# The start of a hybrid attention, convolution and expert block: small loads between tiles of x, first transposes over six banks

## The chip, the cores and the metric

The kernel runs on one core of one Trainium2 chip. The metric is the device time of one execution in microseconds (us). Three executions of the kernel before took 1255.04, 1256.41 and 1256.52 us; the median is 1256.41.

## What is computed

The input x has 512 rows of 1024 float32. With random weights, one layer computes:

```python
h = rmsnorm(x, g_mix)
proj = h @ w_in                      # 1024 x 4608: q | k | v | GLU input | branch gates
o = diff_attention(q, k, v, lam, rel_bias)      # 4 heads, two softmax maps each, chunk-causal
u = glu_a * sigmoid(glu_b); u = silu(layernorm(depthwise_conv31(u)))
merged = gate_A * (rmsnorm(o) @ w_attn_up) + gate_B * (u @ w_conv_pw2 + b_conv_pw2)
x = x + merged @ w_out
x = x + hier_moe(rmsnorm(x, g_ffn))  # 64 experts: top group of 8, top 2 of 8 in it, SwiGLU
out = rmsnorm(x, g_final)
```

## The kernel before

The five engines and their queues have programs of their own, each in a fixed order written by hand, and they meet by semaphores. x lies in four tiles of 128 rows by 1024. A dense part (projection, attention, convolution, merge, output projection) comes first, then the expert part, which streams the weights of the experts (2 MB for each of gate, up and down) through three places in SBUF. These places overlap memory that the dense part uses, so the first loads of expert weights wait for tiles of the dense part; `load_first(0, 0)` waits for the last tile of the output projection.

The change is in the first 30 us. What happens there, engine by engine:

- SP (L565 on) issues the loads: four tiles of x (L568), then six small vectors (`VEC_ROWS`: g_mix, b_conv_pw2, b_dw, g_conv_ln, b_conv_ln, g_subln) into `rows29` (L573), the convolution taps `w_dw` (L575) and `rel_bias` (L576). Then the first chunk of w_in, `glu_b` (2 MB, L587), the rest of `consts` (L589), four lambda vectors (L591) and the second chunk, `glu_a`. All of it is one queue. ACT issues the identity, `consts[:, 0:P]`, itself (L751).
- VectorE and ScalarE compute the mean square of two tiles of x each (L1026, L759), ScalarE the roots (L764), VectorE the scaled rows `xn` (L1032, `xn_ready`).
- TensorE (L1497 on) waits for the identity and for all eight small loads, transposes the small vectors and taps (tile `vec`, L1500 and L1502), which VectorE copies to `vec` and `taps` (L1041 to L1045). Then it transposes `xn` into hT: eight columns of 128 features, each four transposes of 128 by 128, one PSUM bank for a column (tile `xT`, c). Columns 0 and 1 are done tile by tile as `xn` comes (L1518), columns 2 to 7 one after the other (L1524). The banks rotate over three (`NBANK`, `open_tile`): tile n of the plan `PLAN` takes bank n % 3 and waits until tile n - 3 has been copied out. After column 5 stand the two bias rows (`bias_rows`, L1508 to L1512), which need `consts` and `rel_bias` and write into the two banks of `ps_s`.
- ScalarE copies each column, times g_mix and rounded, to `hT` (L783, `hT_high`); after column 2 stands `high_part(0)`, which rounds the first piece of `glu_b` (L777) and waits for its load. `high_part(1)` and the copy of the bias rows follow after column 7.
- VectorE computes the remainder `hT_low` of each column (L1049), which frees the bank.
- GpSimd subtracts the rounded piece of weights from the raw one (L693, `w_split`).
- TensorE then runs the projection tiles (`split_columns`, matmuls at L1492): for each 24 matmuls of 128 x 128 by 128 x 512, in three passes (high times high, low times high, high times low), eight columns in each. The first tile (n == 0) waits column by column.

After the eight GLU tiles come the strips of the bias, q, k, v, then the gates between the steps of the attention.

Of the kernel before, what the change touches and what calls it, by code (L numbers as in the profile page):

```python
# [30 lines left out]
ALU = mybir.AluOpType  # L31
# [3 lines left out]
P = 128  # L35
# [121 lines left out]
def plan():  # L157

    tiles = [("vec", 0)]
    tiles += [("xT", c) for c in range(KD)]  # L160
    tiles += GLU + [("strip", h) for h in range(HEADS)]
    tiles += [("q", m) for m in range(HEADS)] + [("k", m) for m in range(HEADS)]
    tiles += [("v", t) for t in range(T)]
    for m in range(2 * KD):
        tiles.append(("gate", m))
        if m == 5:
            tiles.append(("mean", 0))
        if m == 8:
            tiles.append(("var", 0))
    tiles += [("yc", 0), ("yc", 1)] + [("oT", h) for h in range(HEADS)]  # L170
    for m in range(KD):
        tiles += [("yc", m + 2)] * (m < KD - 2) + [("ya", m)]
    for t in range(T):
        tiles += [("out", 2 * t), ("out", 2 * t + 1)]
        if t:
            tiles += [("hT", 2 * t - 2), ("hT", 2 * t - 1)]
    tiles += [("hT", 2 * T - 2), ("hT", 2 * T - 1)]
    return tiles
# [52 lines left out]
def block_kernel(nc, a, out):  # L231
# [5 lines left out]
    with ExitStack() as ctx:  # L237
# [174 lines left out]

        def xT_bank(n):
            return (pair_a, pair_b)[n // 2 % 2][:, n % 2, :]
# [7 lines left out]
        in_const, in_const2, in_small, in_bcast = sem("in_const"), sem("in_const2"), sem("in_small"), sem("in_bcast")  # L422
        in_x = [sem(f"in_x{t}") for t in range(T)]
# [142 lines left out]
        def _(sp):  # L566
            for t in range(T):
                sp.dma_start(x[:, t, :], ap("x")[0, t * P:(t + 1) * P, :]).then_inc(in_x[t], 16)  # L568
# [7 lines left out]
            sp.dma_start(rb_sb[:, :], ap("rel_bias")).then_inc(in_small, 16)  # L576
# [166 lines left out]
        def _(act_e):  # L743
# [37 lines left out]
            for c in range(KD):  # L781
                tile_ready(act_e, "xT", c)
                act_e.activation(hT[:, c, :], bank_of("xT", c)[:, :], ACT.Copy,  # L783
                                 scale=vec[:, VEC["g_mix"] + c:VEC["g_mix"] + c + 1]).then_inc(hT_high, 1)
                if c == 2:
                    high_part(0)
# [225 lines left out]
        def _(dve):  # L1012
# [24 lines left out]
            for t in range(1, T):  # L1037
                scale_x(t)
# [8 lines left out]
            for c in range(KD):  # L1047
                dve.wait_ge(hT_high, c + 1)
                dve.scalar_tensor_tensor(out=hT_low[:, c, :], in0=bank_of("xT", c)[:, :],  # L1049
                                         scalar=vec[:, VEC["g_mix"] + c:VEC["g_mix"] + c + 1], in1=hT[:, c, :].bitcast(F32),  # L1050
                                         op0=ALU.mult, op1=ALU.subtract).then_inc(copied("xT", c), 1)
# [412 lines left out]
        def _(pe):  # L1464
# [9 lines left out]
            def split_columns(kind, m, n):  # L1474

                dst = open_tile(kind, m)
                name, j = PIECES[n]
# [6 lines left out]
                for i, (w, rows) in enumerate(passes):  # L1484
                    if n == 0 and i == 1:
                        pe.wait_ge(w_split, 1)
                    for c in range(KD):
                        if n == 0 and i == 0:
                            pe.wait_ge(hT_high, c + 1)
                        if n == 0 and i == 2:  # L1490
                            tile_out(pe, "xT", c)
# [6 lines left out]
            pe.wait_ge(in_small, 16 * (len(VEC_ROWS) + 2))  # L1498
# [7 lines left out]
            def bias_rows():  # L1506

                pe.wait_ge(in_const2, 16)  # L1508
                at, w = CONST["bucket"]
# [4 lines left out]
            first = [open_tile("xT", c) for c in range(2)]  # L1514
            for t in range(T):
                pe.wait_ge(xn_ready, t + 1)
                for c in range(2):
                    last = pe.transpose(first[c][:, t * P:(t + 1) * P], xn[:, t, c * P:(c + 1) * P], ident)  # L1518
                    if t == T - 1:
                        last.then_inc(tile_done, 1)  # L1520
            for c in range(2, KD):
                dst = open_tile("xT", c)
                for t in range(T):
                    last = pe.transpose(dst[:, t * P:(t + 1) * P], xn[:, t, c * P:(c + 1) * P], ident)  # L1524
                last.then_inc(tile_done, 1)
                if c == 5:
                    bias_rows()
# [395 lines left out]
```

## Time and profile before

| | |
|---|---|
| median of three executions | 1256.41 us (1255.04 to 1256.52) |
| the profiled execution | 1256.11 us, span 1254.3 us |
| PE (matmul) busy | 1116.5 us, 89% of the span |
| DVE busy | 562.6 us, 45% |
| ACT busy | 271.4 us, 22% |
| POOL busy | 143.0 us, 11% |
| DMA | 408.83 MB, mean 326 GB/s |

The span runs from the first to the last instruction of the profiled execution. PE is TensorE's matmul, PEld its weight load, DVE VectorE, ACT ScalarE, POOL GpSimd, SPq the issue of DMAs by SyncE. Busy shares are means over a program whose parts have different limits: in the first slice PE waits for its inputs, then it is busy almost without a break, and in the later two thirds of the span DMA moves around 425 GB/s.

### The profile page before, as it was taken

How to read it: one execution, taken by the hardware profiler on the slowest of the kernel's cores; microseconds unless marked ns; L12 is line 12 of the kernel's file. 1: busy time of each engine (PE TensorE's matmuls, PEld its weight loads, DVE VectorE, ACT ScalarE, POOL GpSimd, SP SyncE). 2: the span in 40 equal slices, each digit the busy share in tenths (PEclk: the TensorE clock that was granted, in tenths of full speed). 3: DMA queues.
4: the chain of work that ended last, by engine and by line, in shares of the span. 5: the costliest groups of instructions: out<-in, count | busy, mean ns of one | idle time of the engine just before them, and what ended most of it. 6: DMA issues, size and time to landing. Idle time of an engine off the chain costs nothing.

```text
span 1254.3 us, 29895 instructions
## 1 busy us (share of the span) xinstructions
PE 1116.5 (89%) x12369; PEld 684.0 (55%) x12370; DVE 562.6 (45%) x1176; ACT 271.4 (22%) x683; POOL 143.0 (11%) x84
## 2 busy tenths in 40 slices
PE   5999999999999987689997999997998877796886
PEld 4878777768885544345553555544554433353444
DVE  3799433545245542334443444443443433242342
ACT  4133234385132110111111111111111111011112
POOL 2454543246100000000000000000000000000000
PEclk9999999999999998889998999998999989898899
DMA  6333111153159999999999999999999999999995
GB/s 238 118 99 114 68 67 68 68 201 125 78 206 370 425 422 424 426 427 381 393 426 425 426 425 425 424 425 425 427 425 426 426 425 425 423 426 427 425 423 239
DMA packets 51309, 408.83 MB, mean 326 GB/s; under 512 B 6410, under 2 KB 6567, under 8 KB 21066
## 3 DMA queue, kind: packets, MB, share of 16 engines
q1 hardware_dynamic: 50778, 407.22, 78.4%
q0 software_dynamic: 352, 1.06, 0.3%
q8 instruction: 25, 0.41, 0.1%
q10 hardware_dynamic: 144, 0.07, 0.0%
q14 instruction: 10, 0.08, 0.0%
HBM read 406.22 MB, written 2.11 MB: 326 GB/s over the span
## 4 chain that ended last, share of the span: by engine, by line
DMA 64%; PE 29%; ACT 2%; DVE 2%; issue 1%; SPq 1%; DVEq 0%; ACTq 0%
DMA sb_weights<-in_w_exp_up 60%; PE ps_all L1492 13%; DMA sb_weights<-in_w_exp_gate 3%; PE ps_all L1736 2%; PE ps_all L1543 2%; PE ps_all L1670 1%; PE ps_all L1674 1%; PE ps_all L1667 1%; DMA sb_consts<-in_consts 1%; PE ps_all L1622 1%; PE ps_all L1795 1%; PE ps_all L1628 1%; PE ps_all L1625 1%; PE ps_all L1557 1%; PE ps_all L1863 1%
## 5 line engine op out<-in xcount | busy, mean ns | idle before, releaser
L1736 PE MATMUL ps_all<-sb_weights,sb_late 128*32 128x256 f32 x4608 | 306.4, 421 | 89.2 <-DMA sb_weights<-in_w_exp_up 87.8
L1736 PEld LDWEIGHTS ps_all<-sb_weights,sb_late 128*32 128x32 f32 x4608 | 168.2, 117 | 218.9 <-issue 133.7
L1397 DVE TENSOR_TENSOR sb_late<-sb_late,ps_all 128x128 f32<-128x128 f32 x72 | 20.7, 288 | 392.9 <-ACT sb_late L970 392.9
L1392 DVE TENSOR_TENSOR sb_x<-sb_x,ps_all 128x512 f32<-128x512 f32 x184 | 114.1, 682 | 105.1 <-PE ps_all L1795 105.1
L1749 PE MATMUL ps_all<-sb_weights,sb_late 128*32 128x256 f32 x2304 | 139.2, 382 | 0.4 <-ACT sb_late L974 0.4
L1717 PE MATMUL ps_all<-sb_hT,sb_late 128*32 128x256 f32 x2304 | 138.5, 380 | 0.6 <-DVE sb_late L1266 0.6
L1492 PE MATMUL ps_all<-sb_hT_r,sb_ring_r 128*128 128x512 f32 x512 | 124.0, 394 | 0.0
L1492 PEld LDWEIGHTS ps_all<-sb_hT_r,sb_ring_r 128*128 128x128 f32 x512 | 94.8, 188 | 26.8 <-issue 6.5
L1717 PEld LDWEIGHTS ps_all<-sb_hT,sb_late 128*32 128x32 f32 x2304 | 75.7, 109 | 61.0 <-issue 17.4
L1749 PEld LDWEIGHTS ps_all<-sb_weights,sb_late 128*32 128x32 f32 x2304 | 67.5, 109 | 63.3 <-issue 25.6
L970 ACT ACTIVATE sb_late<-ps_all 128x128 f32<-128x128 f32 x72 | 20.0, 278 | 366.7 <-PE ps_all L1736 366.7
L1795 PE MATMUL ps_all<-sb_g_ffn,sb_late 32*128 32x512 f32 x736 | 87.2, 587 | 0.0
L693 POOL TENSOR_TENSOR sb_ring_r<-sb_ring,sb_ring_r 128x1024 fp32r<-128x1024 f32 x32 | 76.3, 2394 | 66.5 <-ACT sb_ring_r L777 65.5
L1064 DVE SCALAR_TENSOR_TENSOR ps_all<-sb_work,sb_taps,ps_all 128x512 f32<-128x512 f32 x116 | 79.7, 749 | 1.2
L962 ACT ACTIVATE sb_late<-ps_all 128x256 f32<-128x256 f32 x72 | 27.7, 384 | 176.9 <-PE ps_all L1717 176.9
L980 ACT ACTIVATE sb_late<-ps_all 128x256 f32<-128x256 f32 x72 | 27.7, 385 | 173.6 <-PE ps_all L1749 173.6
L1492 PE MATMUL ps_all<-sb_x_r,sb_ring_r 128*128 128x512 f32 x256 | 63.2, 389 | 0.0
L1795 PEld LDWEIGHTS ps_all<-sb_g_ffn,sb_late 32*128 32x128 f32 x736 | 37.7, 185 | 41.3 <-issue 41.3
L1381 DVE SCALAR_TENSOR_TENSOR ps_all<-sb_late,sb_consts 128x512 f32<-128x512 f32 x72 | 54.2, 753 | 0.0
L1492 PEld LDWEIGHTS ps_all<-sb_x_r,sb_ring_r 128*128 128x128 f32 x256 | 48.1, 188 | 10.0
L1795 PE MATMUL ps_all<-sb_router_w,sb_late 32*128 32x512 f32 x368 | 52.5, 640 | 0.0
L1724 PE MATMUL ps_all<-sb_consts,sb_late 128*128 128x128 f32 x144 | 31.4, 300 | 17.0 <-ACT sb_late L962 16.8
(307 smaller groups left out, 1058.7 us busy)
## 6 DMA issues: line engine op xcount, KB each, us to landing
sb_weights<-in_w_exp_up SPq DMA_DIRECT2D x59, 2048.0 KB, 14.6
sb_weights<-in_w_exp_down SPq DMA_DIRECT2D x59, 2048.0 KB, 14.5
sb_weights<-in_w_exp_gate SPq DMA_DIRECT2D x59, 2048.0 KB, 14.5
sb_ring<-in_w_in SPq DMA_DIRECT2D x9, 2048.0 KB, 9.0
sb_x<-in_x SPq DMA_DIRECT2D x8, 512.0 KB, 5.1
sb_ring<-in_w_conv_pw SPq DMA_DIRECT2D x1, 2048.0 KB, 9.1
sb_ring<-in_w_attn_up SPq DMA_DIRECT2D x1, 2048.0 KB, 7.8
sb_ring<-in_w_out SPq DMA_DIRECT2D x1, 2048.0 KB, 12.8
```

Source lines behind the costliest of these rows:

```text
L693: pool.tensor_tensor(w_low[name][:, :, j * P:(j + 1) * P], raw, high.bitcast(F32), ALU.subtract).then_inc(w_split, 1)
L962: act_e.activation(rows_sb, ps_rows[:, 0:QCOLS], ACT.Copy).then_inc(rows_ready, 1)
L980: act_e.activation(y_sb[c], ps_y[:, 0:QCOLS], ACT.Copy).then_inc(y_ready, 1)
L1064: dve.scalar_tensor_tensor(out=dst, in0=pad[:, c, k:k + SEQ], scalar=taps[:, c, k:k + 1], in1=conv_sum[c], op0=ALU.mult, op1=ALU.add).then ...
L1381: dve.scalar_tensor_tensor(out=ps_second, in0=d_list[:, 1, :], scalar=slot_at, in1=w_list[:, 1, :], op0=ALU.is_equal, op1=ALU.mult).then_i ...
L1392: ins = dve.tensor_tensor(rows, rows, banks[g].rearrange("p (t s) -> p t s", t=T), ALU.add)
L1492: last = mm(dst[:, :], w[:, c, :], rows[:, c, :], start=i + c == 0, stop=i == 2 and c == KD - 1)
L1717: last = mm(ps_rows[g * BLK:(g + 1) * BLK, 0:QCOLS], onehots[c][:, t, :], h2[:, t, g * QCOLS:(g + 1) * QCOLS], start=t == 0, stop=t == T - 1)
L1724: last = pe.transpose(ps_hTb[:, c * P:(c + 1) * P], rows_sb[:, c * P:(c + 1) * P], ident)
L1736: last = mm(ps_gu[g * BLK:(g + 1) * BLK, 0:2 * P].rearrange("p (a n) -> p a n", a=2), rows, weights[:, at:at + 3:2, r % 4, cols], start=r ...
L1749: last = mm(ps_y[g * BLK:(g + 1) * BLK, 0:QCOLS], actT[:, k * BLK:(k + 1) * BLK], weights[:, 6 * c + 4 + k // 2, k % 2 * 2 + g // 2, g % 2 ...
L1795: last = mm(banks[g], y_sb[j][rows, half * P:(half + 1) * P], w_rows[j][rows, :], start=j == 0, stop=j == NBUF - 1)
```

## The change

Three things are moved. SP issues x0 and x1, then the six vectors and the taps, then x2, x3 and rel_bias, which gets a semaphore of its own (`in_rb`). The transposes of x no longer belong to the plan of rotating tiles: six columns have a bank each (`hx_bank`), and the transposes of columns 0 to 5 run tile by tile as `xn` comes; columns 6 and 7 follow in the banks of columns 0 and 1 once these are lowered (`hT_lowered`). Semaphores `hx_done` and `hT_lowered` take the place of the tile counters. `bias_rows` stands after all the transposes and waits for `in_rb` and for `hT_lowered` 5, since columns 3 and 4 lie in the banks that it writes. The second projection tile waits for `hT_lowered` 8. All later tiles of the plan have numbers lower by eight, so their banks are others.

```diff
--- before.py
+++ after.py
@@ -157,7 +157,6 @@
 def plan():
 
     tiles = [("vec", 0)]
-    tiles += [("xT", c) for c in range(KD)]
     tiles += GLU + [("strip", h) for h in range(HEADS)]
     tiles += [("q", m) for m in range(HEADS)] + [("k", m) for m in range(HEADS)]
     tiles += [("v", t) for t in range(T)]
@@ -410,6 +409,8 @@
             return pairs[t].rearrange("p a n -> p (a n)")
 
 
+        hx_bank = [ps_t, ps_o, ps_oT, ps_s[:, 0, :], ps_s[:, 1, :], bank[2], ps_t, ps_o]
+
         def xT_bank(n):
             return (pair_a, pair_b)[n // 2 % 2][:, n % 2, :]
 
@@ -420,6 +421,7 @@
 
 
         in_const, in_const2, in_small, in_bcast = sem("in_const"), sem("in_const2"), sem("in_small"), sem("in_bcast")
+        in_rb, hx_done, hT_lowered = sem("in_rb"), sem("hx_done"), sem("hT_lowered")
         in_x = [sem(f"in_x{t}") for t in range(T)]
         in_ring = [sem(f"in_ring{i}") for i in range(NRING)]
         in_router = sem("in_router")
@@ -564,7 +566,7 @@
 
         @block.sync
         def _(sp):
-            for t in range(T):
+            for t in range(2):
                 sp.dma_start(x[:, t, :], ap("x")[0, t * P:(t + 1) * P, :]).then_inc(in_x[t], 16)
             at = 0
             for name, rows in VEC_ROWS:
@@ -573,7 +575,9 @@
                 sp.dma_start(rows29[at:at + rows, :], ap(src)[0].rearrange("(r p) -> r p", p=P)).then_inc(in_small, 16)
                 at += rows
             sp.dma_start(taps_row, ap("w_dw")[0]).then_inc(in_small, 16)
-            sp.dma_start(rb_sb[:, :], ap("rel_bias")).then_inc(in_small, 16)
+            for t in range(2, T):
+                sp.dma_start(x[:, t, :], ap("x")[0, t * P:(t + 1) * P, :]).then_inc(in_x[t], 16)
+            sp.dma_start(rb_sb[:, :], ap("rel_bias")).then_inc(in_rb, 16)
             for n, name in enumerate(CHUNKS):
                 before = [c for c in CHUNKS[:n] if PLACE[c] == PLACE[name]]
                 if name == "up":
@@ -779,8 +783,8 @@
 
             act_e.wait_ge(vec_ready, 1)
             for c in range(KD):
-                tile_ready(act_e, "xT", c)
-                act_e.activation(hT[:, c, :], bank_of("xT", c)[:, :], ACT.Copy,
+                act_e.wait_ge(hx_done, c + 1)
+                act_e.activation(hT[:, c, :], hx_bank[c], ACT.Copy,
                                  scale=vec[:, VEC["g_mix"] + c:VEC["g_mix"] + c + 1]).then_inc(hT_high, 1)
                 if c == 2:
                     high_part(0)
@@ -1034,7 +1038,8 @@
             square_x(0)
             scale_x(0)
             square_x(2)
-            for t in range(1, T):
+            scale_x(1)
+            for t in range(2, T):
                 scale_x(t)
 
             tile_ready(dve, "vec", 0)
@@ -1046,9 +1051,9 @@
 
             for c in range(KD):
                 dve.wait_ge(hT_high, c + 1)
-                dve.scalar_tensor_tensor(out=hT_low[:, c, :], in0=bank_of("xT", c)[:, :],
+                dve.scalar_tensor_tensor(out=hT_low[:, c, :], in0=hx_bank[c],
                                          scalar=vec[:, VEC["g_mix"] + c:VEC["g_mix"] + c + 1], in1=hT[:, c, :].bitcast(F32),
-                                         op0=ALU.mult, op1=ALU.subtract).then_inc(copied("xT", c), 1)
+                                         op0=ALU.mult, op1=ALU.subtract).then_inc(hT_lowered, 1)
 
             dve.wait_ge(in_bcast, 64)
             for j in range(2):
@@ -1474,6 +1479,8 @@
             def split_columns(kind, m, n):
 
                 dst = open_tile(kind, m)
+                if n == 1:
+                    pe.wait_ge(hT_lowered, KD)
                 name, j = PIECES[n]
                 low, high = w_low[name][:, :, j * P:(j + 1) * P], high_of(n)
                 passes = [(high, hT), (low, hT), (high, hT_low)]
@@ -1488,14 +1495,14 @@
                         if n == 0 and i == 0:
                             pe.wait_ge(hT_high, c + 1)
                         if n == 0 and i == 2:
-                            tile_out(pe, "xT", c)
+                            pe.wait_ge(hT_lowered, c + 1)
                         last = mm(dst[:, :], w[:, c, :], rows[:, c, :],
                                   start=i + c == 0, stop=i == 2 and c == KD - 1)
                 last.then_inc(tile_done, 1)
 
 
             pe.wait_ge(in_const, 16)
-            pe.wait_ge(in_small, 16 * (len(VEC_ROWS) + 2))
+            pe.wait_ge(in_small, 16 * (len(VEC_ROWS) + 1))
             dst = open_tile("vec", 0)
             pe.transpose(dst[:, 0:NVEC], rows29, ident[0:NVEC, 0:NVEC])
             for c in range(KC):
@@ -1506,25 +1513,25 @@
             def bias_rows():
 
                 pe.wait_ge(in_const2, 16)
+                pe.wait_ge(in_rb, 16)
+                pe.wait_ge(hT_lowered, 5)
                 at, w = CONST["bucket"]
                 mm(ps_s[0:HEADS, 0, :], rb_sb[:, :], consts[0:BUCKETS, at:at + SEQ], start=True, stop=True)
                 mm(ps_s[0:HEADS, 1, 0:P], rb_sb[:, :], consts[0:BUCKETS, at + SEQ:at + w], start=True, stop=True)\
                     .then_inc(rb_done, 1)
 
-            first = [open_tile("xT", c) for c in range(2)]
             for t in range(T):
                 pe.wait_ge(xn_ready, t + 1)
-                for c in range(2):
-                    last = pe.transpose(first[c][:, t * P:(t + 1) * P], xn[:, t, c * P:(c + 1) * P], ident)
+                for c in range(6):
+                    last = pe.transpose(hx_bank[c][:, t * P:(t + 1) * P], xn[:, t, c * P:(c + 1) * P], ident)
                     if t == T - 1:
-                        last.then_inc(tile_done, 1)
-            for c in range(2, KD):
-                dst = open_tile("xT", c)
+                        last.then_inc(hx_done, 1)
+            for c in range(6, KD):
+                pe.wait_ge(hT_lowered, c - 5)
                 for t in range(T):
-                    last = pe.transpose(dst[:, t * P:(t + 1) * P], xn[:, t, c * P:(c + 1) * P], ident)
-                last.then_inc(tile_done, 1)
-                if c == 5:
-                    bias_rows()
+                    last = pe.transpose(hx_bank[c][:, t * P:(t + 1) * P], xn[:, t, c * P:(c + 1) * P], ident)
+                last.then_inc(hx_done, 1)
+            bias_rows()
 
             for n, (name, m) in enumerate(GLU):
                 split_columns(name, m, n)
```

## Rows read from the trace of the kernel before

**Rows 1.** The page, part 4: shares of the chain that ended last.

```profile
DMA 64%; PE 29%; ACT 2%; DVE 2%; issue 1%; SPq 1%; DVEq 0%; ACTq 0%
```

**Rows 2.** The chain in time (start us, us, what), 0 to 70, then 345 to 420.

```profile
6.33 12.82 DMA sb_consts<-in_consts
...
21.46 43.56 PE ps_all L1492 x192
...
359.52 7.68 DMA sb_weights<-in_w_exp_gate
```

**Rows 3.** Timeline (start us, us, engine, line, ...), SP's DMA issues.

```profile
0.72 1.82 SPq L568 DMA_DIRECT2D sb_x<-in_x  x4
...
2.58 0.40 SPq L573 DMA_DIRECT2D sb_late<-in_g_mix  x1
...
5.21 0.25 SPq L575 DMA_DIRECT2D sb_late<-in_w_dw  x1
...
5.87 0.42 SPq L587 DMA_DIRECT2D sb_ring<-in_w_in  x1
```

**Rows 4.** The same timeline, ScalarE.

```profile
6.16 1.06 ACT L759 ACTIVATE sb_dense<-sb_x 128x1024 f32<-128x1024 f32 x1 [3.40 <-DMA sb_x<-in_x]
...
9.17 1.06 ACT L759 ACTIVATE sb_dense<-sb_x 128x1024 f32<-128x1024 f32 x1 [1.49 <-DMA sb_x<-in_x]
...
14.73 1.84 ACT L783 ACTIVATE sb_hT_r<-ps_all,sb_vec 128x512 fp32r<-128x512 f32 x3 [4.04 <-PE ps_all L1518]
...
17.13 1.06 ACT L777 ACTIVATE sb_ring_r<-sb_ring 128x1024 fp32r<-128x1024 f32 x1 [0.56 <-DMA sb_ring<-in_w_in]
18.10 1.83 ACT L783 ACTIVATE sb_hT_r<-ps_all,sb_vec 128x512 fp32r<-128x512 f32 x3
...
21.06 1.27 ACT L783 ACTIVATE sb_hT_r<-ps_all,sb_vec 128x512 fp32r<-128x512 f32 x2 [1.13 <-PE ps_all L1524]
```

**Rows 5.** The same timeline, VectorE and TensorE.

```profile
11.60 0.75 DVE L1032 TENSOR_SCALAR sb_dense<-sb_x,sb_small 128x1024 f32<-128x1024 f32 x1
...
12.24 0.28 PE L1500 MATMUL ps_all<-sb_consts,sb_late 29*128 29x29 f32 x1 [12.24 <-DMA sb_rb_sb<-in_rel_bias]
...
12.88 1.97 PE L1518 MATMUL ps_all<-sb_consts,sb_dense 128*128 128x128 f32 x8
12.98 0.19 DVE L1041 COPY sb_vec<-ps_all 128x29 f32<-128x29 f32 x1 [0.63 <-PE ps_all L1502]
...
18.80 2.07 DVE L1049 SCALAR_TENSOR_TENSOR sb_x_r<-ps_all,sb_vec,sb_hT_r 128x512 fp32r<-128x512 f32 x3 [1.28 <-ACT sb_hT_r L783]
...
19.20 1.02 PE L1510 MATMUL ps_all<-sb_consts,sb_rb_sb 32*4 32x512 f32 x2 [0.69 <-DMA sb_consts<-in_consts]
...
20.36 1.09 PE L1524 MATMUL ps_all<-sb_consts,sb_dense 128*128 128x128 f32 x8
...
21.21 3.92 PE L1492 MATMUL ps_all<-sb_hT_r,sb_ring_r 128*128 128x512 f32 x16
...
26.78 3.79 PE L1492 MATMUL ps_all<-sb_hT_r,sb_ring_r 128*128 128x512 f32 x16
...
32.22 3.79 PE L1492 MATMUL ps_all<-sb_hT_r,sb_ring_r 128*128 128x512 f32 x16
```

**Rows 6.** Timeline of TensorE alone, batches of 64 in the expert loop.

```profile
471.46 5.45 PE L1736 MATMUL ps_all<-sb_weights,sb_late 128*32 128x256 f32 x64 [4.96 <-DMA sb_weights<-in_w_exp_up]
...
486.25 6.60 PE L1736 MATMUL ps_all<-sb_weights,sb_late 128*32 128x256 f32 x64 [4.81 <-DMA sb_weights<-in_w_exp_up]
...
950.23 5.11 PE L1736 MATMUL ps_all<-sb_weights,sb_late 128*32 128x256 f32 x64 [4.41 <-DMA sb_weights<-in_w_exp_up]
...
1201.65 5.46 PE L1736 MATMUL ps_all<-sb_weights,sb_late 128*32 128x256 f32 x64 [4.05 <-DMA sb_weights<-in_w_exp_up]
```

**Rows 7.** Windows: us, busy us of each engine, granted clock, DMA share, GB/s.

```profile
471.46:476.90 5.44, 5.44 (x68) 3.27 (x72) 0.00 (x0) 0.00 (x0) 0.00 (x0) 0.69 1.02 429
...
570.21:574.06 3.85, 3.85 (x68) 2.37 (x68) 0.00 (x0) 0.39 (x1) 0.00 (x0) 1.00 0.97 409
```

## The prediction

> **What bounds the kernel now.** I read the shares of the chain of waits first, then the chain in order of time, then the timeline of the first 50 us. By shares the chain is 64% DMA and 29% PE [rows 1]: the experts' weights stream at the DMA limit, the dense part before them is TensorE. In order of time [rows 2] the chain has the load of consts until 19.15, and then PE without a break: 43.56 us of projection matmuls from 21.46 on. Where the output matmuls end, at 359.52, the chain passes to the first load of expert weights, and from there it is nearly all transfers. So what the change does to the moment at which PE gets through the first projection tile is passed on in full: PE has no idle time that could absorb it, and the stream of weights starts when PE's dense work ends. The routing is by data, so the number of loads stays.
>
> In the first 27 us, four engines work side by side [rows 3 to 5]. SP issues four tiles of x, seven small loads and rel_bias, then glu_b at 5.87. PE stands until 12.24 for the last small load, then transposes. ACT starts copying hT at 14.73, does three columns, waits for glu_b until 17.13, splits its first piece (1.06), and goes on. PE meets consts at 19.20 (two bias rows), transposes the last two columns at 20.36, starts the first projection tile at 21.21 and the second at 26.78, where an undisturbed tile takes 32.22 - 26.78 = 5.44.
>
> **The change part by part.**
>
> *Small loads between x1 and x2.* Two x issues take 0.91 of the 1.82; the small ones run from 2.58 to 5.46 (2.88 us). So x2 is issued at about 4.5 instead of 1.6 and x3 at 5.0 instead of 2.1; rel_bias and glu_b keep their place, as do consts, the lambdas and the next chunk behind them. Do x2 and x3 land later? x1 landed at 6.16 and x3 at 9.17 [rows 4], 1.5 us a tile, so the queue was still at x1 when x2 will be issued. Nothing is later at the lower end; at the upper end the full 2.88 us. I take 0 (the row of x1 is near, and the bytes ahead of glu_b are the same), 0.5 being possible. The small loads are then in at about 7.5 and the vec transposes leave the path; before, they stood at 12.24 with 0.64 us to the first transpose.
>
> *Six banks, tile by tile.* VectorE gives the last tile of x at 11.60 + 0.75 = 12.35 [rows 5], and the vec copies queued behind it, 0.38 us from 12.98 on, end at about 12.75. With eight transposes in 1.76 us (12.88 to 14.64), 0.22 each, six cost 1.3 a tile; the first three tiles lie beside VectorE's work, the last ends at 13.2 to 14.4, and column 0 is ready at 12.9 to 13.5 instead of 14.73. So ACT starts 1.2 to 1.8 us earlier. That gain is worth nothing: after three columns (until 14.7 to 15.3) ACT's next instruction in order is the split of glu_b, whose transfer still lands at 17.1, and columns 3 to 7 are queued behind it. What is gained there is one later stall: ACT no longer waits 1.13 us for columns 6 and 7 (21.06), so columns 3 to 7 run 18.10 to 21.1 at 0.60 each instead of ending at 22.33.
>
> *bias_rows behind all transposes, with a new wait for hT_lowered 5.* Columns 3 and 4 are in banks of ps_s. VectorE lowers column 3 from 18.80 and column 4 by 18.80 + 2 x 0.69 = 20.18. So the bias rows, now the last thing ahead of the first projection, start at 20.2 instead of 19.20. Queued behind the wait are the whole projection stream and everything that depends on it. They take 1.16 us (19.20 to 20.36), and the first projection starts at 21.36, not 21.21: +0.15. The two columns of transposes (0.85) that stood between now lie beside ACT. The first tile took 5.57 before, with small stalls for columns 6 and 7; these columns are now ready, and it takes 5.44: -0.13. Sum so far 0.0. The added wait of the second projection tile for hT_lowered 8 (about 21.9) is long met at 26.8; renumbering the tiles moves their banks by one and keeps the distance of three.
>
> *PE idles before the bias rows.* Its last transposes (column 7, after VectorE lowered column 1) end at 15.6 to 16.6, the next work is at 20.2: 3.6 to 4.6 us of idle time where the kernel before waited 0.69. What such a gap does is shown in the expert loop [rows 6, 7]: a batch of 64 matmuls takes 3.85 at a granted clock of 1.00 (570.21), but 5.45 after 4.96 us of idle (471.46), with a mean clock of 0.69, so part of it runs at 1.2 instead of 2.4 GHz. There are 17 such batches, the first at 471.46 and the last at 1201.65, each after 4.05 us of idle or more; the shortest is 5.11, the longest 6.60, their mean 5.62. No gap of 4.05 us or more was free of it. The bias rows and the first projection tile are such dense work, so the loss is 1.3 to 2.8 us, by the mean 1.8. This is the only term of size. Lower end: nothing, if the gap is too short.
>
> The transposes before were at full speed by 20.36: eight in 1.09 there against 1.97 at 12.88, though they had nothing but transposes ahead [rows 5]. The Trainium skill (TensorE: Matmul & The Clock Gate, Part 4: PE-mode transpose) says that transposes do not count as activity for the full clock. By that rule the first projection tile of the kernel before would have started at 1.2 GHz as well, the change would lose nothing new, and the sum would be 0.0. The trace does not agree: 16 projection matmuls from 21.21 on took 3.92 us, about the 3.8 of the later tiles.
>
> Sum: 0.0 + 1.8 on the profiled execution's 1256.11 (span 1254.3 and 1.8 around it) is 1257.9; that execution is 0.3 under the median shown, 1256.41, so 1258.2.
>
> **The rivals.**
>
> A, the forecast: all gains hidden behind glu_b, +1.8 from the clock. 1258.2, own range 1257.5 to 1259.5.
>
> B, the clock stays up. The gap can be 3.6 us, shorter than any that the trace shows to cost. Then nothing changes in sum: 1256.4. For it: the length. Against: every gap only half a microsecond longer had it fall [rows 6], and the transposes ahead of this one leave PE idle between tiles as well. This is also what the skill's rule on transposes would give.
>
> C, slower: the late x2 and x3 are the bound. If the queue runs dry between x1 and x2, x3 slips by up to 2.88 us. From 1.8 us of slip on (17.13 less the 15.3 at which ACT ends three columns) this decides also without the loads behind it; what glu_b and consts slip counts in full from the first tenth. With all of it 1256.4 + 2.9 + 1.8 = 1261.1, with a slip of 1 us 1259.2. Against: DMA was still delivering x1 at 6.16.
>
> D, faster: glu_b or consts land earlier because fewer small packets stand in their way at that time. ACT then starts its split at 15.3 instead of 17.13, columns 3 to 7 end at 19.3, bias rows start at 18.4, 1.8 us earlier, after an idle time too short for the clock: 1254.6. For it: ACT and PE really are ready earlier, so this is the one thing that would cash the 1.2 to 1.8 us. Against: the same bytes stand ahead of glu_b in the same queue.
>
> **How the numbers follow.** About 0.2%, 2.5 us, is what a measurement of this kernel can tell from no change. A 0.55, B 0.2, C 0.13, D 0.12. The likeliest gives 1258.2. The range 1255.0 to 1260.5 leaves out the ends of C and D. Slower by over 0.2% (above 1258.9): a quarter of A, the long cold stretches, and nearly all of C, 0.25. Faster (below 1253.9): half of D and some chance on top for a mechanism that I do not see, 0.08. Same: 0.67. The expert loop adds its own scatter of a microsecond or so: the batch at 1201.65, near the end, is one of those that took from 5.11 to 6.60.
>
> **What would show it.** The vec transposes before 9 us; the first hT activation at 13 to 13.5, three of them, then the wait for glu_b to about 17.1; columns 3 to 7 in one run to 21.1; bias rows at about 20.2 after 3.6 us or more of idle PE; the first 16 projection matmuls in 5 us or more, not 3.92; the second projection tile at 28.5, not 26.78; the first load of expert weights at 361.3, not 359.52. Full clock in these 16 matmuls means B. x3 landing after 9.7 or glu_b after 17.6 means C, glu_b before 16.5 means D. The forecast is wrong if the second tile starts before 27 or after 30, or if the load of expert weights does not move with it.

## The result, and the profile after

The changed kernel takes 1260.48 us (median of 8 executions, 1258.77 to 1261.06), the kernel before 1256.21 (8 executions, 1254.53 to 1256.93). The ratio is 1.0029 with a 95% interval of 1.0020 to 1.0038: slower by 4.3 us by the medians, clear of noise. The profiled execution has a span of 1257.5 us, 3.2 more than before.

The chain in order of time (start us, us, what), from the start and around 360 us. Where [rows 2] had the load of consts, there is now the load of x2; from it the chain goes on over VectorE, the transposes and ScalarE to column 4 on VectorE (ready at 20.56) and the bias rows. The projection block that took 43.56 takes 46.32; the first load of expert weights stands at 362.88 instead of 359.52.

```profile
3.97 6.21 DMA sb_x<-in_x
...
22.55 46.32 PE ps_all L1499 x192
...
362.88 7.74 DMA sb_weights<-in_w_exp_gate
```

SP's issues, which answer to [rows 3]. The seven small loads now stand between 1.64 and 3.97; x2 and x3 follow. The seven issues take 2.29 us here and took 2.88 before, where one of them alone had 0.73, so x2 goes out 0.5 us earlier than counted.

```profile
0.72 0.87 SPq L570 DMA_DIRECT2D sb_x<-in_x  x2
...
1.64 0.37 SPq L575 DMA_DIRECT2D sb_late<-in_g_mix  x1
...
3.97 0.83 SPq L579 DMA_DIRECT2D sb_x<-in_x  x2
```

ScalarE, answering to [rows 4]. The second tile that ACT squares is in hand at 11.51 instead of 9.17, the first three columns of hT start at 15.74 instead of 14.73, the split of glu_b follows them without a wait at 17.46 (17.13 before), and the five other columns run in one piece.

```profile
11.51 1.06 ACT L763 ACTIVATE sb_dense<-sb_x 128x1024 f32<-128x1024 f32 x1 [4.29 <-DMA sb_x<-in_x]
...
15.74 1.85 ACT L787 ACTIVATE sb_hT_r<-ps_all,sb_vec 128x512 fp32r<-128x512 f32 x3 [2.71 <-PE ps_all L1526]
...
17.46 1.06 ACT L781 ACTIVATE sb_ring_r<-sb_ring 128x1024 fp32r<-128x1024 f32 x1
18.41 3.01 ACT L787 ACTIVATE sb_hT_r<-ps_all,sb_vec 128x512 fp32r<-128x512 f32 x5
```

VectorE and TensorE, answering to [rows 5]. The vec transposes come 3 us earlier (9.25), but the last tile of xn only at 13.94 + 0.75 = 14.69 (12.35 before). After column 7 (its last transpose ends at 18.57) PE is idle for 2.12 us until VectorE has lowered column 4. Then the bias rows take 1.42 instead of 1.02, and 16 projection matmuls take 6.49 instead of 3.92. The second tile starts at 30.63 instead of 26.78, the third 5.44 later, as before.

```profile
9.25 0.28 PE L1507 MATMUL ps_all<-sb_consts,sb_late 29*128 29x29 f32 x1 [9.25 <-DMA sb_late<-in_w_dw]
...
13.94 0.75 DVE L1036 TENSOR_SCALAR sb_dense<-sb_x,sb_small 128x1024 f32<-128x1024 f32 x1
...
17.26 1.31 PE L1532 MATMUL ps_all<-sb_consts,sb_dense 128*128 128x128 f32 x8 [0.56 <-DVE sb_x_r L1054]
...
19.14 3.38 DVE L1054 SCALAR_TENSOR_TENSOR sb_x_r<-ps_all,sb_vec,sb_hT_r 128x512 fp32r<-128x512 f32 x5 [0.61 <-ACT sb_hT_r L787]
...
20.70 1.42 PE L1519 MATMUL ps_all<-sb_consts,sb_rb_sb 32*4 32x512 f32 x2 [2.12 <-DVE sb_x_r L1054]
...
22.48 6.49 PE L1499 MATMUL ps_all<-sb_hT_r,sb_ring_r 128*128 128x512 f32 x16
...
30.63 3.79 PE L1499 MATMUL ps_all<-sb_hT_r,sb_ring_r 128*128 128x512 f32 x16
...
36.07 3.79 PE L1499 MATMUL ps_all<-sb_hT_r,sb_ring_r 128*128 128x512 f32 x16
```

Windows of the same execution (busy us of PE, PEld, DVE, ACT, POOL, then granted clock, DMA share, GB/s). Before the bias rows PE is busy for 0.58 of 2.70 us. In the first projection tile the granted clock is 0.50, that is 1.2 GHz, and in the third window it comes back. Narrower windows put the fall at about 21.2, inside the bias rows, and the return at 28.0.

```profile
18.00:20.70 2.70, 0.58 (x7) 0.37 (x6) 2.09 (x4) 2.70 (x6) 2.09 (x1) 1.00 0.93 351
22.48:26.00 3.52, 3.52 (x9) 2.81 (x9) 2.50 (x5) 0.74 (x2) 2.40 (x1) 0.50 0.39 146
26.00:29.00 3.00, 3.00 (x10) 2.38 (x9) 0.00 (x0) 2.00 (x2) 1.08 (x1) 0.67 0.01 2
```

### The profile page after: what moved, and what is told of

The parts are those of the page before. It is cut to its first block, busy times and chain, and to the rows that moved or that the text cites. A ratio compares the mean times of both kernels' runs of the same rounds, so it can differ in the third digit from the quotient of the medians.

```text
span 1257.5 us, 29896 instructions
## 1 busy us (share of the span) xinstructions
PE 1119.4 (89%) x12369; PEld 685.5 (55%) x12370; DVE 564.5 (45%) x1176; ACT 271.3 (22%) x683; POOL 143.0 (11%) x84
## 3 DMA queue, kind: packets, MB, share of 16 engines
HBM read 406.22 MB, written 2.11 MB: 325 GB/s over the span
## 4 chain that ended last, share of the span: by engine, by line
DMA 64%; PE 29%; DVE 2%; ACT 2%; issue 1%; SPq 1%; POOL 0%; DVEq 0%; ACTq 0%
DMA sb_weights<-in_w_exp_up 60%; PE ps_all L1499 13%; DMA sb_weights<-in_w_exp_gate 3%; PE ps_all L1743 2%; PE ps_all L1550 2%; PE ps_all L1677 1%; PE ps_all L1681 1%; PE ps_all L1674 1%; PE ps_all L1632 1%; PE ps_all L1802 1%; PE ps_all L1635 1%; PE ps_all L1629 1%; PE ps_all L1564 1%; PE ps_all L1870 1%; PE ps_all L1756 1%
## 5 line engine op out<-in xcount | busy, mean ns | idle before, releaser
L1499 PE MATMUL ps_all<-sb_hT_r,sb_ring_r 128*128 128x512 f32 x512 | 126.6, 400 | 0.0
```

The lines of the kernel that those rows point to most:

```text
L1499: last = mm(dst[:, :], w[:, c, :], rows[:, c, :], start=i + c == 0, stop=i == 2 and c == KD - 1)
```

## The experiments

Each was timed beside the kernel before. A useful mark is the start of the second projection tile: from there to the first load of expert weights the twelve profiles have 332.2 to 333.6 us, whatever was changed ahead of it, and from that load to the end 893.8 to 895.7.

```
kernel                    median   ratio to before (95%)     2nd tile  expert load
before                    1256.2                             26.78     359.52
changed                   1260.5   1.0029 (1.0020-1.0038)    30.63     362.88
e1 loads only             1258.3   1.0014 (1.0005-1.0023)    27.54     361.10
e2 banks only             1260.6   1.0034 (1.0022-1.0047)    31.59     363.93
e3 gap filled             1257.0   1.0003 (0.9994-1.0012)    27.57     360.91
e4 small loads on ACT     1264.6   1.0061 (1.0047-1.0075)    33.48     367.00
e5 bias rows later        1256.6   0.9999 (0.9990-1.0008)    26.87     359.42
e6 before, bias later     1257.2   1.0006 (0.9997-1.0014)    27.50     360.04
e7 x first, vec later     1256.8   0.9999 (0.9990-1.0008)    26.93     360.19
e8 e7, reordered, filled  1258.0   1.0009 (1.0000-1.0018)    27.16     360.40
e9 gaps filled in place   1254.3   0.9982 (0.9973-0.9991)    25.44     357.85
e10 e9 without filling    1257.9   1.0009 (1.0000-1.0018)    26.86     359.91
```

The medians are of several sessions; the kernel before had medians of 1256.2 to 1257.0 in them, so the ratios are what to compare. The two marks are of one profiled execution each, and that need not be a typical one: between the changed kernel and e3 the second tile moves by 3.06 us, the load of expert weights by 1.97 and the ratio by 0.0026, which is 3.3 us.

**e1: only the order of the loads**, in the kernel before.

```diff
-            for t in range(T):
+            for t in range(2):
                 sp.dma_start(x[:, t, :], ...)
...
+            for t in range(2, T):
+                sp.dma_start(x[:, t, :], ...)
+            sp.dma_start(rb_sb[:, :], ap("rel_bias")).then_inc(in_rb, 16)
```

> The kernel before with only the order of the loads changed (x0, x1, small, x2, x3, rel_bias); banks, transposes and bias rows as before. Theory (late x and a half-rate clock together make the loss, the clock the larger part): the last tile of xn comes at about 14.7 instead of 12.35, column 0 of hT at 15.7 or so, bias rows at 19.2 to 20, PE has no gap of 2 us ahead of them, the clock stays up; the second projection tile starts at 27.0 to 27.8, and the time is 0.3 to 1.2 us above the kernel before. Rival (the order of the loads is the whole loss): 3 to 4 us above it. Second rival (the clock falls in any case): the first 16 projection matmuls take 5 us or more.

Measured: 1.0014, second tile at 27.54, 0.76 later than before. Its timeline:

```profile
15.29 1.84 ACT L786 ACTIVATE sb_hT_r<-ps_all,sb_vec 128x512 fp32r<-128x512 f32 x3 [2.29 <-PE ps_all L1522]
...
16.82 2.82 PE L1528 MATMUL ps_all<-sb_consts,sb_dense 128*128 128x128 f32 x12 [0.50 <-DVE sb_x_r L1052]
...
19.57 1.40 PE L1514 MATMUL ps_all<-sb_consts,sb_rb_sb 32*4 32x512 f32 x2
...
21.97 3.92 PE L1495 MATMUL ps_all<-sb_hT_r,sb_ring_r 128*128 128x512 f32 x16
...
27.54 3.79 PE L1495 MATMUL ps_all<-sb_hT_r,sb_ring_r 128*128 128x512 f32 x16
```

Column 0 starts at 15.29 and not at 14.73, because x2 and x3 are late here too. PE has almost no gap, and the 16 projection matmuls take 3.92. But twelve transposes from 16.82 on take 2.82, and the bias rows at 19.57 still 1.40, where they took 1.02 at 19.20 before: with the early work spread thin the clock also came up later. The bias rows start 0.37 later and their first product takes 0.38 longer, which is nearly all of the 0.76. The rows of the granted clock show 1.00 in this stretch, so the later rise is read from the durations alone. The order of the loads costs, but it is not the whole. By the ratio it costs more than the mark says, 1.8 us with an interval of 0.6 to 2.9, and more than the 0.3 to 1.2 that I expected.

**e2: only the banks and the bias rows**, in the changed kernel with all of x loaded first.

```diff
-            for t in range(2):
+            for t in range(T):
                 sp.dma_start(x[:, t, :], ...)
...
-            for t in range(2, T):
-                sp.dma_start(x[:, t, :], ...)
```

> The changed kernel with the order of the loads put back: all of x first, then the small loads. Six banks, the new place of the bias rows and their wait stay. The vec transposes and with them all transposes of x wait until about 12 for the small loads, then 24 in a row take 5.3 us at the price before, so column 0 is ready at about 17 and the bias rows start at 21 to 22. Theory (the loss is mostly the clock after a gap of PE): PE is now busy from 12 to 18 and the gap before the bias rows is again 2 to 3 us, so the clock falls in some or all executions; 2 to 4 us above the kernel before. Rival (late x2 and x3 are the loss): no more than 1.5 us above it.

Measured: 1.0034, some 4.3 us and so a little above the forecast of 2 to 4, second tile at 31.59.

```profile
12.28 5.38 PE L1524 MATMUL ps_all<-sb_consts,sb_dense 128*128 128x128 f32 x24
...
16.69 1.84 ACT L785 ACTIVATE sb_hT_r<-ps_all,sb_vec 128x512 fp32r<-128x512 f32 x3 [6.74 <-PE ps_all L1524]
...
21.65 1.86 PE L1517 MATMUL ps_all<-sb_consts,sb_rb_sb 32*4 32x512 f32 x2 [2.11 <-DVE sb_x_r L1052]
...
23.87 6.06 PE L1497 MATMUL ps_all<-sb_hT_r,sb_ring_r 128*128 128x512 f32 x16
...
31.59 3.79 PE L1497 MATMUL ps_all<-sb_hT_r,sb_ring_r 128*128 128x512 f32 x16
```

With the small loads behind all of x, PE starts x only at 12.28, and runs 24 transposes in a row (5.38), 19 of them ahead of the copy of column 0 (16.69). The gap before the bias rows is 2.11 us, and again the first projection tile runs at half rate (6.06). So with the vec transposes in front of those of x, six banks need the small loads early; and with early or late x the gap and the clock are the same.

**e3: the gap filled.** Nine matmuls of the identity with itself, into the bank that the first projection tile takes next. The trace shows a float32 product of this kind as two records, so nine are x18, and the two bias rows are x2 at L1519 and x2 at L1520.

```diff
+            for _ in range(9):
+                mm(bank[1][:, 0:P], ident, ident, start=True, stop=True)
             bias_rows()
```

> The changed kernel with nine 128x128 matmuls of the identity into an unused bank between the last transposes of x and the bias rows, some 2.1 us of work in the gap of 2.1. Theory: the clock stays at 2.4 GHz, the first 16 projection matmuls take 3.8 to 4 us instead of 6.49, the second projection tile starts at 28 instead of 30.63, and the time is 2.2 to 3 us below the changed kernel, 1 to 1.7 above the kernel before. Rival (the wait for hT_lowered and late x are the whole loss, the reduced clock is a symptom): no faster than the changed kernel, within 0.5 us.

Measured: 1.0003, from 1260.5 to 1257.0, second tile at 27.57.

```profile
18.55 2.17 PE L1535 MATMUL ps_all<-sb_consts 128*128 128x128 f32 x18
...
20.84 1.01 PE L1519 MATMUL ps_all<-sb_consts,sb_rb_sb 32*4 32x512 f32 x2
...
22.00 3.92 PE L1499 MATMUL ps_all<-sb_hT_r,sb_ring_r 128*128 128x512 f32 x16
...
27.57 3.79 PE L1499 MATMUL ps_all<-sb_hT_r,sb_ring_r 128*128 128x512 f32 x16
```

Everything up to 20.84 is as in the changed kernel, 0.14 later, and nothing waits less. Yet the bias rows take 1.01 and the 16 matmuls 3.92. Extra work made the kernel 3.5 us faster by the medians and 3.3 by the ratios, so the reduced clock is a cause and not a symptom. From the start of the bias rows to the second tile the changed kernel takes 30.63 - 20.70 = 9.93 us and e3 takes 27.57 - 20.84 = 6.73: the clock costs 3.20 there. What remains of the 3.85 against the kernel before is 0.65 (in e3 itself 0.79, with the 0.14 by which it came later). That this is near the 0.76 of e1 proves nothing, since the paths differ: in e3 the bias rows wait for column 4, in e1 they follow slow transposes.

**e4: the small loads on ACT's queue**, meant to take away the late landing of x2 and x3 alone.

```diff
-            for t in range(2):
+            for t in range(T):
                 sp.dma_start(x[:, t, :], ...)
...
             act_e.dma_start(consts[:, 0:P], ...)
+                act_e.dma_start(rows29[at:at + rows, :], ...).then_inc(in_small, 16)
...
+            act_e.dma_start(taps_row, ap("w_dw")[0]).then_inc(in_small, 16)
```

> The changed kernel with x0 to x3 in a row on SP's queue, and the seven small loads issued by ACT behind the identity; takes away the late landing of x2 and x3 and nothing else. Theory: x3 lands at 9.2 to 9.6, the last xn at 12.4, three columns of hT from about 13.5 on, then ACT waits for glu_b until about 17.1, bias rows at 20.2 instead of 20.70, the clock still falls: 0.5 us below the changed kernel and no more (0 to 1). Rival (late x is the loss): 2 to 4 us below it, level with the kernel before.

Measured: 1.0061, second tile at 33.48. It missed its aim, and both expectations are wrong.

```profile
3.55 0.27 ACTq L753 DMA_DIRECT2D sb_late<-in_w_dw  x1
...
9.18 1.06 ACT L761 ACTIVATE sb_dense<-sb_x 128x1024 f32<-128x1024 f32 x1 [1.87 <-DMA sb_x<-in_x]
...
13.81 0.28 PE L1505 MATMUL ps_all<-sb_consts,sb_late 29*128 29x29 f32 x1 [13.81 <-DMA sb_late<-in_w_dw]
```

x3 was in hand at 9.18, as expected. But w_dw, issued at 3.55, was in only at 13.81, 10 us later, so PE could not start before. It tells nothing about late x; it shows that here the second queue did not carry a small load past the large ones of the first.

**e5: the bias rows behind the first projection tile**, in the changed kernel.

```diff
-            bias_rows()
-
             for n, (name, m) in enumerate(GLU):
                 split_columns(name, m, n)
+                if n == 0:
+                    bias_rows()
```

> The changed kernel with the two bias rows moved from ahead of the first projection tile to behind it. It takes away the wait for hT_lowered 5 ahead of the projection and so the gap of 2.1 us in front of it. Theory (the gap before the bias rows and the clock that falls in it are the loss): the first projection tile starts at 18.5 to 19, its first pass is held by column 7 (ready at 21.4), and if the clock stays up the second tile starts at 26.3 instead of 30.63, that is 4 us below the changed kernel and level with or 0.5 below the kernel before. The one doubt is that eight matmuls spread over 18.6 to 21.5 are too little for the clock: then 28 to 29, 1.5 to 2.5 us below the changed kernel. Rival (the late tiles of x or the new banks are the loss): 0 to 1 us below the changed kernel.

Measured: 0.9999, second tile at 26.87, as before the change.

```profile
18.75 5.21 PE L1499 MATMUL ps_all<-sb_hT_r,sb_ring_r 128*128 128x512 f32 x16
...
26.87 3.94 PE L1499 MATMUL ps_all<-sb_hT_r,sb_ring_r 128*128 128x512 f32 x16
```

Late x, six banks and the early transposes are all still there; only the two bias rows and their wait have moved, and 3.76 us come back at the second tile, 3.9 in the medians. The first projection tile starts at 18.75, its first pass is held by the columns of hT, and the clock stays up.

**e6: the same move in the kernel before.**

```diff
-                if c == 5:
-                    bias_rows()
...
                 split_columns(name, m, n)
+                if n == 0:
+                    bias_rows()
```

> The kernel before with the same move of the bias rows behind the first projection tile. They waited there for consts until 19.20 and held the transposes of columns 6 and 7. Theory: columns 6 and 7 are transposed by 19, ACT copies them at 19.9 to 21.15 without its wait of 1.13 us, the second tile starts at 26.1 instead of 26.78, and the time is 0.5 to 1 us below the kernel before. Rival (consts is not what holds it, the chain of waits only names it): no change.

Measured: 1.0006, no gain; the second tile is at 27.50 instead of 26.1.

```profile
19.35 1.31 PE L1524 MATMUL ps_all<-sb_consts,sb_dense 128*128 128x128 f32 x8 [0.85 <-DVE sb_x_r L1049]
...
26.33 1.02 PE L1510 MATMUL ps_all<-sb_consts,sb_rb_sb 32*4 32x512 f32 x2
...
27.50 3.94 PE L1492 MATMUL ps_all<-sb_hT_r,sb_ring_r 128*128 128x512 f32 x16
```

The first tile does start earlier, 20.66 against 21.21, but no more than that, since columns 6 and 7 wait for the banks of columns 3 and 4 until 19.35, and the 1.17 us of the bias rows now stand between the tiles. The wait for consts in [rows 5] looked like a cost of 0.69 us and hid a wait for banks. Beside e5, with the bias rows in the same place in both, the changed loads and banks are 0.63 us ahead at the second tile (26.87 against 27.50); by the ratios, 0.9999 and 1.0006, that is not clear of noise.

**e7: all of x first, the vec transposes behind those of x, the bias rows behind the first tile.**

```diff
-            dst = open_tile("vec", 0)
-            pe.transpose(dst[:, 0:NVEC], rows29, ident[0:NVEC, 0:NVEC])
...
             for t in range(T):
...
+            dst = open_tile("vec", 0)
+            pe.transpose(dst[:, 0:NVEC], rows29, ident[0:NVEC, 0:NVEC])
...
             for c in range(6, KD):
```

> The changed kernel with all of x loaded first as before, the transposes of the small loads moved behind the transposes of x (columns 0 to 5), and the bias rows behind the first projection tile. So the tile by tile transposes run as xn comes (8.2, 10.1, 11.0, 11.8) and nobody waits for the small loads on PE before they are in. Theory: column 0 of hT is copied from 13.5 to 14.2 on, ACT then waits for glu_b to 17.1, columns 3 to 7 end at 21.2, the second tile starts at 26.2: all that the early transposes gain is lost in the wait for glu_b, 0 to 0.7 us below the kernel before if the clock stays up, 1.5 to 3 above it if the gap from about 16.5 to 18.3 lets it fall. Rival (an early column 0 is worth its 1 to 3 us): 1.5 us or more below the kernel before.

Measured: 0.9999, second tile at 26.93.

```profile
8.33 1.51 PE L1516 MATMUL ps_all<-sb_consts,sb_dense 128*128 128x128 f32 x6 [8.33 <-DVE sb_dense L1034]
...
10.25 3.05 PE L1516 MATMUL ps_all<-sb_consts,sb_dense 128*128 128x128 f32 x18 [0.40 <-DVE sb_dense L1034]
...
14.17 1.84 ACT L785 ACTIVATE sb_hT_r<-ps_all,sb_vec 128x512 fp32r<-128x512 f32 x3 [4.30 <-DVE sb_small L1045]
...
15.70 1.97 PE L1530 MATMUL ps_all<-sb_consts,sb_dense 128*128 128x128 f32 x8 [1.98 <-DVE sb_x_r L1052]
...
17.03 1.06 ACT L779 ACTIVATE sb_ring_r<-sb_ring 128x1024 fp32r<-128x1024 f32 x1 [1.01 <-DMA sb_ring<-in_w_in]
...
18.14 5.88 PE L1497 MATMUL ps_all<-sb_hT_r,sb_ring_r 128*128 128x512 f32 x16 [0.47 <-ACT sb_ring_r L779]
...
26.93 3.94 PE L1497 MATMUL ps_all<-sb_hT_r,sb_ring_r 128*128 128x512 f32 x16
```

Column 0 is copied from 14.17, 1.6 us earlier than in the changed kernel, and the split of glu_b is still at 17.03, behind a wait of 1.01 for its load. So the early column 0 is worth no more than the 0.43 us by which this split is ahead of the changed kernel's (17.46), which was a step of the prediction. Here the first projection tile begins at the lower clock (16 matmuls in 5.88; granted clock 0.50 from 15.70 to 21.70), after PE stood 1.98 us ahead of column 6. My expectation for a fallen clock, 1.5 to 3 us above the kernel before, was too high: the time is level with it.

**e8: e7 with five columns ahead of glu_b, another order of passes, nine idle matmuls behind column 7.**

```diff
-                if c == 2:
+                if c == 4:
                     high_part(0)
...
-                passes = [(high, hT), (low, hT), (high, hT_low)]
+                passes = [(high, hT), (low, hT), (high, hT_low)] if n else [(high, hT), (high, hT_low), (low, hT)]
...
+            for _ in range(9):
+                mm(bank[1][:, 0:P], ident, ident, start=True, stop=True)
             for n, (name, m) in enumerate(GLU):
```

> As the one with vec behind the transposes, and besides ACT does five columns of hT ahead of the first piece of glu_b instead of three, the first projection tile does high times low second and the pass with the low weights last, and nine 128x128 matmuls of the identity stand in the gap of PE. Theory: columns 0 to 4 fill ACT's wait for glu_b, column 7 is ready at 20 instead of 21.2, the first tile ends at 24 to 24.5, the second starts at 25.2 to 25.7 behind the bias rows: 1 to 1.6 us below the kernel before. Rival (glu_a, in at 26.3, and its split bound the third tile anyway): 0 to 0.5 us below it.

Measured: 1.0009, second tile at 27.16, worse than forecast.

```profile
17.57 3.01 PE L1534 MATMUL ps_all<-sb_consts 128*128 128x128 f32 x18
...
20.33 2.10 PE L1497 MATMUL ps_all<-sb_hT_r,sb_ring_r 128*128 128x512 f32 x8
```

The clock had fallen before the idle matmuls (granted 0.50 from 15.95 on), which then took 3.01 us instead of 2.17 and held the first tile until 20.33. In this place the filling saves nothing: e10, the same kernel without it, has the same ratio of 1.0009 and its second tile at 26.86.

**e9: the idle matmuls where PE is idle**, nine ahead of column 6 and four behind column 7.

```diff
+            for _ in range(9):
+                mm(bank[1][:, 0:P], ident, ident, start=True, stop=True)
             for c in range(6, KD):
...
+            for _ in range(4):
+                mm(bank[1][:, 0:P], ident, ident, start=True, stop=True)
             for n, (name, m) in enumerate(GLU):
```

> As the last one, but the idle matmuls stand where PE is idle: nine between the vec transposes and column 6 (a gap of 2.0 us), four behind column 7 (a gap of about 1 us). In the last one the clock fell at 16.1 and the nine matmuls behind column 7 took 3.0 us and held the first projection tile until 20.33. Theory: the clock stays up, the first projection tile starts at 18.2 to 18.6, ends at 23.7 to 24.2, the bias rows behind it, the second tile starts at 25.0 to 25.5 instead of 26.78: 1.3 to 1.9 us below the kernel before. Rival (something later, glu_a or the split of its pieces, bounds the third tile): the second tile is early but the third is not, 0 to 0.5 us below.

Measured: 0.9982 (0.9973 to 0.9991), 1254.3 against 1257.0 of the kernel before in the same session: faster than both kernels. It holds all of x first, six banks, the vec transposes behind those of x, five columns ahead of glu_b, the low weights last in the first tile, the bias rows behind it, and the two fillings.

```profile
13.92 2.27 PE L1528 MATMUL ps_all<-sb_consts 128*128 128x128 f32 x18
...
18.43 2.23 PE L1497 MATMUL ps_all<-sb_hT_r,sb_ring_r 128*128 128x512 f32 x8 [0.26 <-ACT sb_ring_r L779]
...
25.44 3.94 PE L1497 MATMUL ps_all<-sb_hT_r,sb_ring_r 128*128 128x512 f32 x16
```

**e10: e9 without any of them.**

```diff
-            for _ in range(9):
-                mm(bank[1][:, 0:P], ident, ident, start=True, stop=True)
...
-            for _ in range(4):
-                mm(bank[1][:, 0:P], ident, ident, start=True, stop=True)
```

> The same without any idle matmuls. Theory: the clock falls in the gap behind the vec transposes, at about 16, and is back at about 19.5 or 23, so the first projection tile, from 18.2 on, loses 0.6 to 2.4 us: the second tile starts at 25.6 to 27.4, 0.5 to 2.4 us above the one with the gaps filled. Rival (idle matmuls are not what holds the clock): the same time as that one.

Measured: 1.0009; 3.6 us above e9 in the medians, more than the 0.5 to 2.4 that I expected, and 1.42 at the second tile of the profiled execution. First the eight transposes of columns 6 and 7 in e8, then the same in e10 and what follows:

```profile
15.83 1.94 PE L1530 MATMUL ps_all<-sb_consts,sb_dense 128*128 128x128 f32 x8 [1.97 <-DVE sb_x_r L1052]
...
15.67 1.31 PE L1530 MATMUL ps_all<-sb_consts,sb_dense 128*128 128x128 f32 x8 [1.98 <-DVE sb_x_r L1052]
...
18.55 3.58 PE L1497 MATMUL ps_all<-sb_hT_r,sb_ring_r 128*128 128x512 f32 x8 [1.56 <-ACT sb_ring_r L779]
...
26.86 3.94 PE L1497 MATMUL ps_all<-sb_hT_r,sb_ring_r 128*128 128x512 f32 x16
```

The first eight projection matmuls take 3.58 instead of 2.23. Up to column 7, e8 and e10 are the same program for PE, and PE waits 1.97 and 1.98 us ahead of column 6. Yet in e8 the granted clock is at 0.50 from 15.95 on, and in e10 it stays at 1.00 until 18.20 and falls before the first tile starts at 18.55. So the same idle time is not followed by the same stretch of lower clock in every execution. The profiled execution of e10 is also the fastest of its eleven (1256.38 us; the median is 1257.9), so the others may have lost more to the clock; they have no trace, and that this is the reason was not shown.

## Why the prediction was right in its direction and short in its size

The forecast was 1258.2, +1.8 us, as the likeliest; measured are +4.3 us by the medians and 3.85 at the second tile, inside the range by 0.02 us (1260.48, the range ended at 1260.5). That it is inside is luck: two terms of the sum were too small, and a sign that I had named for a wrong forecast, the second tile starting after 30, came (30.63). A change beyond 0.2% upwards, which this is, had a chance of 0.25; I had held no measurable change to be likelier.

*All early gains hidden behind glu_b*: right where it could be tested. In the changed kernel there was no early gain to hide: column 0 could have come at 13 and came at 15.74, and the small loads were in at 9.25 and not at 7.5. e7 gave the early column 0, and the split of glu_b still began at 17.03.

*bias_rows late, +0.15, and the first tile -0.13*: the mechanism was right. The bias rows start at 20.70, not 20.2, another 0.50: the three columns, late with x2, pushed the split of glu_b from 17.13 to 17.46 and columns 3 and 4 behind it (0.33), and the rest is the handing over of column 4, ready on VectorE at 20.56. With the clock kept up (e3) the first tile starts at 22.00 and takes 5.57, as before the change, so the small stalls stayed and the -0.13 did not come.

*The clock*: right in kind, mis-sized. The step took 1.8 us, the mean of 17 batches of the expert loop. It was 3.20 (e3), above their longest, 2.8. From the start of the bias rows to the first tile it is 1.78 against 1.16, in the tile 8.15 against 5.57: 0.62 and 2.58. So the tile alone is near the longest batch, [rows 6] 6.60, and the bias rows, which I had priced at the full rate, come on top. The granted clock was 1.00 in the gap and 0.50 in all of 22.48 to 26.00: it fell when PE was already at work again.

*The gap of 3.6 to 4.6 us*: wrong. It was 2.12, because the last transposes, late with x, ran from 17.26 to 18.57 and not to 15.6 or 16.6. Rival B rested on gaps shorter than 4.05 being harmless, and the forecast on the gap being about 4; e3 and e5 show that half of that did harm. The forecast of a fallen clock came true with a gap that it had not counted on.

*x2 and x3 not late*: wrong, and this was the term taken at 0 with 0.5 allowed. x3 was in hand at 11.51 instead of 9.17, 2.34 late of the 2.88 possible. The argument that the queue was still at x1 held for x1, but x2 goes out at 3.97 and is in at 10.21, 6.2 us later. The price is small, 0.33 at the split of glu_b, since most of the slip was free under the wait for glu_b; that part of rival C was right.

*Transposes and the clock*: the conclusion holds, the line shown for it does not carry it. Between the transposes at 12.88 and those at 20.36 stood the two bias rows, ordinary matmuls, so PE had not had "nothing but transposes ahead". e7 settles it, below.

The sum with measured terms, at the second tile: 0.15 for the bias rows as forecast, 0.50 for their later start (0.33 of it late x), 0 for the first tile, 3.20 for the clock, 3.85 in all, which is 30.63 - 26.78. The medians differ by 4.3. Rival A and a part of C hold together; the prediction had kept them apart.

## What to carry to other kernels

Ahead of dense matmuls, look at what PE does in the last few microseconds before them: a small operation that waits for another engine left a gap of 2 us and cost 3 us of reduced clock here, more than anything that the reordering around it gained. Put such an operation behind the first dense tile, or fill the gap where it is, not after it. And when an engine is made early, follow its in-order queue to the next load: what is behind that load does not move.

## What the runs showed of the hardware

A gap of 2.12 us between transposes and bias rows was enough for 1.2 GHz in the tile behind it, in e2 one of 2.11 and in e4 one of 2.12 as well, where the expert loop had shown a loss only behind gaps of 4 us and more. Gaps of 1.98 and 1.97 us with transposes on both sides were followed by 0.50 at once in e7 and e8, and by 1.00 for another 2.5 us in e10; what decides it is open.

Transposes alone raise the clock: in e7 PE did nothing but transposes from 8.33 on, six took 1.51 us at first, and the eighteen from 10.25 on took 3.05, so the later ones ran at the higher rate. The rows of the granted clock show 1.00 for all of this stretch, so this too is read from the durations. It speaks again against the rule of the Trainium skill (TensorE: Matmul & The Clock Gate, Part 4: PE-mode transpose) that transposes do not count; the trace decides.

A small load of 62 KB issued at 3.55 on ACT's queue (e4) was in at 13.81, 10.3 us later. On SP's queue, issued at 4.63 behind all four tiles of x (e2), it was in by 11.64, 7.0 us later, and issued at 3.68 between tiles of x, at 9.25. Beside a full queue of large loads the second queue was slower in this one execution; why is open.
